# Gated linear attention in a two-block transformer kernel: level order, halved gates, two pairs of score banks, norm by token columns

## The reference, cut to what matters

```
log gates:   la_f, la_b        [512 tokens, 256 key channels] per direction
score[i,j] = sum_ch q[i,ch] * k[j,ch] * exp(sum of la_f over j+1..i)      for j < i
           = sum_ch q[i,ch] * k[j,ch] * exp(sum of la_b over i..j-1)      for j > i
           = sum_ch q[i,ch] * k[i,ch]                                     for j = i
o[i]       = sum_j score[i,j] * v[j]
y[i]       = (o[i] * rsqrt(mean(o[i]^2) + eps) * gain) * output gate       per head
```

## Time and profile before

| what | value |
|---|---|
| median of 3 runs | 3111.52 us |
| span of the profiled execution (no other time of it is given) | 3114.8 us |
| PE busy over the span | 2672.6 us (86%) |
| DVE busy over the span | 857.7 us (28%) |
| ACT busy over the span | 624.4 us (20%) |
| end of `odd_front`'s last operation | 2368.66 us |
| first matmul of the GLA stage | 2378.28 us |
| last operation of the GLA stage | 2499.35 us |
| first matmul of the output projection | 2500.59 us |

### The profile page before, as it was taken

One profiled execution on the slowest core, in us unless ns is written; L12 is line 12 of the kernel. 1 busy time (PEld: TensorE's weight loads), 2 busy tenths in 40 slices (PEclk: granted clock), 3 DMA queues, 4 the chain that ended last, 5 costly groups with the idle time before them and its releaser, 6 DMA issues. The chain is left out here.

```text
span 3114.8 us, 43284 instructions
## 1 busy us (share of the span) xinstructions
PE 2672.6 (86%) x17989; PEld 1410.0 (45%) x17989; DVE 857.7 (28%) x1821; ACT 624.4 (20%) x1222; POOL 200.2 (6%) x157
## 2 busy tenths in 40 slices
PE   6999688869999998998889989974997788998993
PEld 4563577433433433445444444432345644444441
DVE  2721465231112112456430000003332643000002
ACT  4411443320100001233111101012221211110112
POOL 0100344210000000001100000001000010000001
PEclk9989799879999999999989999996998988999997
DMA  8114110529999993001469999994204026999996
GB/s 307 54 54 149 31 57 16 199 81 424 422 400 415 415 405 132 18 4 54 157 261 423 428 428 429 428 366 162 79 0 182 1 71 266 424 428 429 429 427 253
DMA packets 109683, 756.02 MB, mean 243 GB/s; under 512 B 20964, under 2 KB 24272, under 8 KB 70496
## 3 DMA queue, kind: packets, MB, share of 16 engines
q1 hardware_dynamic: 106080, 739.24, 58.0%
q0 software_dynamic: 2592, 12.58, 1.0%
q10 hardware_dynamic: 864, 2.10, 0.2%
HBM read 727.92 MB, written 25.97 MB: 242 GB/s over the span
## 5 line engine op out<-in xcount | busy, mean ns | idle before, releaser
L1894 PE MATMUL bank<-ring,expert_in 128*64 128x512 f32 x1536 | 344.6, 603 | 29.8 <-DMA ring<-in_moe_w_up_dram 26.5
L1829 DVE TENSOR_TENSOR hidden<-silu_gate,bank 128x512 f32<-128x512 f32 x32 | 33.7, 1054 | 734.1 <-PE bank L1894 734.1
L1894 PEld LDWEIGHTS bank<-ring,expert_in 128*64 128x64 f32 x1536 | 121.8, 139 | 246.6 <-issue 237.5
L1623 PE MATMUL bank<-ring,expert_in 128*64 128x512 f32 x1024 | 224.8, 597 | 7.2 <-DVE home L1471 5.5
L1905 PE MATMUL bank<-ring,hidden_T 128*64 128x512 f32 x768 | 170.1, 596 | 31.8 <-ACT hidden_T L1853 31.8
L1883 PEld LDWEIGHTS bank<-onehot,x_part 128*128 128x128 bf16 x3072 | 176.3, 99 | 31.4 <-issue 24.3
L1883 PE MATMUL bank<-onehot,x_part 128*128 128x128 bf16 x3072 | 181.8, 222 | 6.8 <-DVE onehot L1820 6.8
L1623 PEld LDWEIGHTS bank<-ring,expert_in 128*64 128x64 f32 x1024 | 73.6, 138 | 156.2 <-issue 141.4
L2620 PE MATMUL bank<-ring,home 128*128 128x512 f32 x256 | 119.2, 628 | 21.6 <-PEq L193 21.6
L553 PE MATMUL bank<-home,ring 128*128 128x512 f32 (+1 forms) x384 | 127.5, 493 | 7.5 <-PEq L193 7.5
L1638 PE MATMUL bank<-ring,hidden_T 128*64 128x512 f32 x512 | 123.9, 646 | 3.7 <-ACT hidden_T L1546 3.7
(11 more groups left out here) (632 smaller groups left out, 3743.8 us busy)
## 6 DMA issues: line engine op xcount, KB each, us to landing
ring<-in_moe_w_gate_dram SPq DMA_DIRECT2D x52, 2048.0 KB, 22.4
ring<-in_moe_w_up_dram SPq DMA_DIRECT2D x50, 2048.0 KB, 27.5
ring<-in_moe_w_down_dram SPq DMA_DIRECT2D x50, 2048.0 KB, 27.9
ring<-in_w_gate_dram SPq DMA_DIRECT2D x32, 2048.0 KB, 13.3
ring<-in_w_up_dram SPq DMA_DIRECT2D x32, 2048.0 KB, 14.6
ring<-in_w_down_dram SPq DMA_DIRECT2D x32, 2048.0 KB, 16.1
ring<-in_w_mod_dram SPq DMA_DIRECT2D x12, 2048.0 KB, 12.7
home<-in_moe_w_down_dram SPq DMA_DIRECT2D x9, 2048.0 KB, 32.6
```

The costliest lines, as they stand in the source:

```text
L1623: mm = pe.matmul(B[2 + 2 * part + b][rows, :], xe[:, dc, rows], ws[e][:, c, b * COLS:(b + 1) * COLS], start=(dc == 0), stop=(dc == NC - 1))
L1894: mm = pe.matmul(B[2 + 2 * part][rows, :], xe[:, c, rows], ws[e][:, c, :], start=(c == 0), stop=(c == NC - 1))
```

## The change: what it does

- The tables are loaded within the stage: two of them (`lt`, `gt`), then the 21 level tables, then the gain, in front of the ring's loads on the same queue. TensorE waits for the two before the first sums and for the others before the second.
- The order is by head pairs: all groups of pair 0, then all of pair 1, with far groups placed between near ones. Sums are issued two units ahead.
- The exponentials are taken by halves, so that ScalarE lays out in one buffer what scales q and in the other what scales k; VectorE then needs two products of 512 columns for a unit.
- ScalarE copies the far scores (`hold`), VectorE masks only near ones. A far group is weighed one group later, behind other work of TensorE.
- For pair 0 the scores alternate between banks 2, 3 and 6, 7 (the second pair's output banks, not yet used). For pair 1 they use banks 2, 3, and from the sixth group on also 4, 5 in alternation.
- Pair 0 is weighed and normed while pair 1 is under way.
- The norm sums by token columns: the squares are the stationary operand and a single column of ones the moving one, so that the sums stand as 128 partitions x 4 columns per head. Root and reciprocal run on 128x8. VectorE makes diagonal matrices from them, and a product with ones spreads them over the partitions again.

```diff
-        load(m, [(seg[:, :, :], m.const_dram[:, len(CONST_NAMES) + 1:, :]), (gain[:, :], columns(I["od_gla_norm_2"][0]))])
-        sq, root = E[:, 0, :, :], E[:, 1, :, :]
+        sq = sb("gla_sq", [P, 2, T])
+        root, inverse = sb("gla_root", [P, 2, 2 * NT]), sb("gla_inverse", [P, 2, 2 * NT])
...
-        units = [(L, c) for L in (7, 8, 0, 1, 2, 3, 4, 5, 6) for c in range(2)]
+        phases = [[(None, 0), (7, 0), (0, 0), (8, 0), (1, 0), (8, 1), (2, 0), (6, 0), (3, 0), (4, 0), (5, 0)],
+                  [(None, 0), (0, 0), (1, 0), (2, 0), (7, 0), (3, 0), (8, 0), (4, 0), (8, 1), (5, 0), (6, 0)]]
+        turn = len(phases[0])
+        groups = [(L, c, part) for c in range(2) for L, part in phases[c]]
...
+        def banks_of(n):
+            k = n % turn
+            if n < turn:
+                return (2, 3) if k % 2 == 0 else (6, 7)
+            return (4, 5) if k >= 5 and k % 2 else (2, 3)
...
+                sp.dma_start(seg[:, 0:first - near, :], m.const_dram[:, at + near:at + first, :]).then_inc(near_here, 16)
+                sp.dma_start(seg[:, first - near:, :], m.const_dram[:, at + first:, :]).then_inc(tables_here, 16)
+                sp.dma_start(gain[:, :], columns(I["od_gla_norm_2"][0]), allow_slow_non_contiguous=True).then_inc(gain_here, 16)
                 m.load_until(sp, upto)
...
+                def totals(c):
+                    pe.wait_ge(squared, 2 * c + 2)
+                    for odd in range(2):
+                        for t in range(NT):
+                            mm = pe.matmul(total_bank(c)[:, odd * NT + t:odd * NT + t + 1], sq[:, odd, t * P:(t + 1) * P], one[:, 0:1],
+                                           start=True, stop=True)
+                def spreads(c):
+                    for odd in range(2):
+                        pe.wait_ge(opposite, 2 * c + odd + 1)
+                        pe.matmul(spread_bank(c, odd)[:, :], one, W[:, c, odd, :, :], start=True, stop=True).then_inc(spread, 1)
...
+                for n in range(len(groups)):
+                    scores(n)
+                    if n == 0:
+                        sums_of(1)
+                    if opens(n) and unit_of[n] + 2 < N:
+                        sums_of(unit_of[n] + 2)
+                    if held_back is not None:
+                        weigh_far(held_back)
+                        held_back = None
+                    if is_far(n):
+                        held_back = n
+                    if n == turn:
+                        weigh_near(0)
+                    if n == turn + 1:
+                        totals(0)
+                    if n == turn + 2:
+                        spreads(0)
+                weigh_near(1)
+                totals(1)
+                spreads(1)
...
-                        act.activation(E[:, x % 2, d, :], m.psum[d][:, :], ACT.Exp).then_inc(exped, 1)
+                        for s, half in ((0, 1 - d), (1, d)):
+                            ins = act.activation(halves(E[:, x % 2, s, :], L)[:, :, half, :], halves(m.psum[d][:, :], L)[:, :, half, :], ACT.Exp)
...
+                for n in range(len(groups)):
+                    if is_far(n):
+                        hold(n)
+                    if opens(n) and unit_of[n] + 2 < N:
+                        exps(unit_of[n] + 2)
+                    if n == turn:
+                        squares(0)
+                    if n == turn + 1:
+                        roots(0)
...
-                    for half in range(2):
-                        for out, of, d in ((qe, gq, 1 - half), (ke, gk, half)):
+                    for s, (out, of) in enumerate(((qe, gq), (ke, gk))):
+                        dve.tensor_tensor(out[:, x % 2, :], of[:, c, :], E[:, x % 2, s, :], ALU.mult).then_inc(gated, 1)
...
+                x = 1
+                for n in range(len(groups)):
+                    if not is_far(n):
+                        mask(n)
+                    while x < N and (x < 2 or last_group[x - 2] <= n):
+                        gates(x)
+                        x += 1
+                    if n == turn:
+                        scale(0)
+                    if n == turn + 1:
+                        diagonals(0)
+                    if n == turn + 2:
+                        norms(0)
+                scale(1)
+                diagonals(1)
+                norms(1)
```

More of the change, by code:

```diff
@@ L3388, in _, with weigh_far @@
-                pe.wait_ge(taken, 2 * n)
-                for h in range(HEADS):
-                    weigh(h // 2, h % 2, lambda at: W[:, h // 2, h % 2, at, :], same[0], True).then_inc(weighed, 1)
-                for h in range(HEADS):
-                    pe.wait_ge(squared, h + 1)
-                    pe.matmul(m.psum[h % 4][:, :], one, sq[:, h % 2, :], start=True, stop=True).then_inc(totalled, 1)
+                def weigh_far(n):
+                    L, c, part = groups[n]
+                    if c == 1 and L == 7:
+                        pe.wait_ge(normed, 2)
+                    for odd in range(2):
+                        pe.wait_ge(held, 2 * far_of.index(n) + 1 + odd)
+                        mm = weigh(c, odd, lambda at: tmp[:, odd, at * P:(at + 1) * P], beyond[L, part])
+                    mm.then_inc(moved, 1)
@@ new lines, in exps, with hold, squares @@
+                        ins.then_inc(exped, 1)
+                def hold(n):
+                    k = far_of.index(n)
+                    act.wait_ge(scored, n + 1)
+                    if k:
+                        act.wait_ge(moved, k)
+                    for odd in range(2):
+                        act.activation(tmp[:, odd, :], m.psum[banks_of(n)[odd]][:, :], ACT.Copy).then_inc(held, 1)
+                def squares(c):
+                    for odd in range(2):
+                        act.wait_ge(weighed, 2 * c + odd + 1)
+                        if c:
+                            act.wait_ge(totalled, c)
+                        act.activation(sq[:, odd, :], m.psum[4 + 2 * c + odd][:, :], ACT.Square).then_inc(squared, 1)
@@ L3418, in _ @@
+                squares(1)
+                roots(1)
             @block.vector
             def _(dve):
-                order = Order(dve, root_order)
-                n_scored = 0
                 def gates(x):
@@ new lines, in mask @@
+                def mask(n):
+                    L, c, _ = groups[n]
+                    k = near_of.index(n)
+                    dve.wait_ge(scored, n + 1)
+                    if L == 0 and c == 0:
+                        dve.wait_ge(tables_here, 16)
+                    if k:
+                        dve.wait_ge(masked, 2 * k)
+                    for odd in range(2):
+                        bank = m.psum[banks_of(n)[odd]][:, :].rearrange("p (t f) -> p t f", t=NT)
+                        if L is None:
+                            ins = dve.tensor_tensor(W[:, c, odd, :, :], bank, over(m.c("ident"), NT), ALU.mult)
+                        else:
+                            ins = dve.copy_predicated(W[:, c, odd, :, :], over(sg(f"cross{L}").bitcast(I32), NT), bank)
+                        ins.then_inc(masked, 1)
```

172 lines of the change are left out of this document (87 added, 85 removed).

## The result

The changed kernel took 3075.56 us (median of 4 runs, 3072.15 to 3078.52) beside 3111.58 us of the kernel before: ratio 0.9881, 95% interval 0.9868 to 0.9893, a gain of 36.0 us where 28.5 were forecast. Two later measurements of the same two kernels gave ratios of 0.9895 (0.9878 to 0.9911) and 0.9899 (0.9883 to 0.9916).

A forecast was written before the change was run, and what follows sets the result against it. TensorE was taken to bound the stage's near stretch. Start 4.4, middle 12.9 less 5.6 and end 16.4 gave 28.1 us; semaphores -0.6 and projection clock +1.1 made 28.5: 3111.5 - 28.5 = 3083.0 us, range 3076 to 3095.

The forecast's parts named there:

- low clock: TensorE at low clock: 5 us at the first sums, costing 2.5 us; 1.5 us more at the stage's end.
- start: Stage's beginning: two tables loaded in front let sums start at 2373.9 instead of 2378.28, 4.4 us gained.
- middle (12.9 less 5.6): First sums to last weighing: 12.9 us gained, less 5.6 us of pair 0's weighing and norm work moved in.
- rival B: Level tables land with the ring's loads, TensorE waits from 2379 to 2404: 3110.5 us, no change; chance 0.04.
- (1): Stall behind level 8's second group, for which later gates wait: 1.5 us once per pair, 3.0 us in all.
- (4): Stall before the last weighing, which waits for the last mask: 1.65 us.
- (2): Stall at pair 1's first group, waiting for the mask of pair 0's last, behind gates: 0.5 us.
- Chain of a unit: Steady near units: gates done 4.1 us after the sums begin, wanted at 5.07, slack 1.0 us; TensorE unbroken.
- Rival A: Sums-to-gates chain becomes the bound if strided halves cost full width: 16 units lose about 0.5 each, 3091 us; chance 0.19.
- Norm: Stage's end, from the last weighing: 8.65 us by the later head, plus 1.5 for low clock and 0.8 for hops.
- Table loads: Two more for pair 0's root between exponentials: charged nothing; with the skill's 1.38 us drain each, 3084.7 us.
- Rival C: Clock stays low in the middle's 14 near units, whose 43 us of work take twice that: 3126 us; chance 0.02.

The follow-up runs named there:

- u_norm: Changed kernel with the sums of squares, root and reciprocal over 128x512 per head again; ratio to the kernel before 0.9936, stage 111.67 us.
- u_turn: Changed kernel with pair 0's near weighing and norm at the end, pair 1's scores in banks 2 and 3 alone; ratio to the kernel before 0.9917, stage 107.48 us.
- u_order: Changed kernel with far groups one after the other instead of between near ones; ratio to the kernel before 0.9911, stage 99.13 us.
- v_best: Changed kernel with pair 0 as in u_order, pair 1's last mask and last far copy beside other TensorE work; ratio to the kernel before 0.9895, stage 96.90 us.
- c_before: The kernel before, unchanged, run again with a new profile; ratio 1.0 (0.999 to 1.0009), stage 131.82 us.
- u_halves: Changed kernel with full-width exponentials and four gate products of 256 columns per unit again; ratio to the kernel before 0.9911, stage 103.33 us.
- u_dvehold: Changed kernel with far scores copied by VectorE, still weighed one group later; ratio to the kernel before 0.9913, stage 107.11 us.

## Why the prediction was right or wrong

The mechanisms stand. The step that failed is the spread between runs, which the range put at nothing: "the forecast's own spread is the totals (-1, +1.5), low clock (-4, +4), hops (+3) and A's end, so 3076 to 3095" has no term for it. The runs showed 15 us between single runs of one kernel, and medians of four runs of the changed kernel that differ by 4.6 us (3075.56, 3077.97, 3080.11). The sizes of the stage's terms were 3.1 us too small in sum, which alone would have stayed inside.

Gains in us, measured as the mean of two traces of before less that of three of the changed kernel ("behind the stage" is from the next stage's first DMA issue to the end of the span):

| step | forecast | measured |
|---|---|---|
| start | 4.4 | 4.8 |
| middle (12.9 less 5.6) | 7.3 | 9.0 |
| end | 16.4 | 17.2 |
| more semaphores | -0.6 | -0.4 |
| behind the stage | 1.1 | 1.6 (single traces 0.9 to 2.7) |
| sum | 28.5 | 32.1 |
| total, 12 and 52 runs | | 33.9 |

- *Start.* Right; the tables landed ahead of the second sums, which carry no wait, so rival B falls.
- *Middle.* Stalls: 5.15 forecast, 4.8 found, each in its place: (1) 2 x 1.56 for 3.0, (4) 1.43 for 1.65, (2) 0.27 for 0.5. Low clock: 2.5 forecast (5 us, half of it lost); found 1.5, 3.1 and 1.5, as the low stretch at the start lasted 3.0, 6.2 and 3.0 us: a mean of 2.0. Work, as TensorE's busy time less that loss: 78.8 forecast, 79.45 - 1.5 = 78.0, 80.92 - 3.1 = 77.8 and 78.0 found, 0.9 less. I took the sums at 1.99 throughout, but the 0.1 us stands only where scores follow; ahead of a weighing, totals or spreads the pitch is 1.89 (2373.49 to 2375.38), seven times. And level 8's sums took 2.87 (2369.53 to 2372.40), not 3.0. Stalls 0.35, low clock 0.5 and work 0.9 make the 1.7 us by which the middle gained more than forecast, the largest error of a term.
- *More semaphores.* 1.58 us for 19 against 1.19 for 12 makes 0.06 each, where 0.086 was taken from the stage with 29.
- *Chain of a unit.* Right: two strided halves end 0.66 to 0.69 us after their start (0.64 forecast), TensorE has no wait in the steady part, and undoing the halves costs 0.3 us of rest. Rival A (full-width price) falls.
- *Norm.* The largest term: 8.65 at full clock plus 2.3 was forecast, 9.1 to 11.0 measured. The three ends took 10.99, 10.30 and 9.13 us at clocks of 0.69, 0.83 and 0.91, so what varies goes with the clock, for which I had 1.5. The terms named there add up to 8.57 by the later head, not 8.65. u_norm puts the column form at 10.3 us, u_turn the overlap of pair 0, shared buffer included, at 6; the prediction gave the second no price of its own.
- *Table loads.* The load at the turn began at 2412.34 us in the trace after and took 1.28; the root began at 2413.63, 0.01 us behind it. The drain of 1.38 us that the Trainium skill, "ScalarE: Activation LUTs", "What ACT_TABLE_LOAD costs", adds is not there, and the 1.7 us by it did not come.
- *Rival C.* The middle has a clock of 0.96 to 0.98. What the Trainium skill, "TensorE: Matmul & The Clock Gate", "A second HAM failure mode: psum-queue depth-cycling", says of short rests did not show at rests of 1.56 us: in three traces the clock was 0.99 or more behind all six. At 1.66 us and above this case has both (see the last section).
- *The part that failed* is in "After" and in "Chances": "The profiled execution has a span of 3114.8, 3.3 us over the median, so the same gain gives 3111.5 - 28.5", and "A run of this kernel tells 0.2%, about 6 us". I had read three runs within 0.3 us as the kernel's spread, and set a span beside times: in each run the time is 1.8 to 2.1 us above the span, so the profiled execution was some 5 us over the median, far outside the three. The lower terms of the range (-1 and -4) reach only 3078; that it went to 3076 has no term behind it.
- *How the error adds up.* Of the 7.5 us in the first measurement 3.1 are the stage's terms and 0.5 lie behind it: with these the forecast would have been 3079.4, inside the range. Another 2.1 are the difference to the later 33.9. The remaining 1.8, between 33.9 and the traces' 32.1, are open. They fit chance ahead of the stage: 3 traces with the old stage begin it at 2357.2 to 2368.7 (mean 2362.8), 13 with some form of the new one at 2354.9 to 2366.0 (mean 2361.7). That the median of the first four runs fell below 3076 was chance; the medians of the other two measurements, and that of all 12 runs (3077.5), lie inside the range.

## What to carry to other kernels

Where an in-order engine is the bound, count its work at full pitch and list its rests one by one; the two sums came out within 1.2% and 0.4 us here. u_order and v_best show that the named idea (alternating levels) was not what removed the rests: work that lies ready at each wait did. A quantity that is repeated over 128 partitions only to be used as a scale belongs in the smallest form before a root and a reciprocal (two reciprocals of 0.20 us in place of four of 3.35). And when the profiled run lies outside the spread of the timed ones, the spread is not yet known: measure the stage in the trace, and widen the range of the total.

## What was unexpected of the hardware

- Identical code reached this stage between 2354.9 and 2368.7 us, and 12 runs of the changed kernel lie between 3069.5 and 3083.5. The time goes with TensorE's mean clock (c_before); what moves the clock from run to run is not known here.
- The length of a rest alone doesn't decide whether the clock falls. Behind all six rests of 1.56 us in the changed kernel's traces it stayed up. In the kernel before, with the clock at 1.00 ahead of them, one rest of 1.66 us was followed by the low clock (3.38 us for 16 records) and two more of 1.66 us were not (2.05); in u_halves one of two rests of 1.69 us was (3.15 for 1.95). Both rests of 2.68 us in u_dvehold were. There TensorE rested 2.3 us longer, and the middle lasted 6.0 us longer.
- Products with one moving column cost 1.78 us for 16 records at full clock (2411.46 to 2413.24), about the same as 16 columns. The 16 weight loads beside them take 1.87 us (2411.35), so it seems to be these that set the pace.
